# Position bias and first modulation as 32-column products, with eight modulation buffers, on one core

## Chip, cores and metric

One core of a Trainium2 chip runs the whole program as one launch. The metric is the device time of that launch in microseconds; lower is better.

## The reference

Two transformer blocks of two layers each, on one sequence of 512 tokens of width 1024. The first block begins, for each layer, with an adaptive modulation; its first attention branch adds a learned bias that depends on the distance of two positions:

```
mod = silu(c) @ w_ada[l] + b_ada[l]            # w_ada[l]: 1024 x 6144
sh1, sc1, g1, sh2, sc2, g2 = split(mod, 6)
h = x * (1.0 + sc1) + sh1
...
bias = rel_bias[t5_bucket(q_pos[:, :, None] - k_pos)]     # 32 buckets, 8 heads
logits = einsum('bqhd,bqkhd->bqkh', q, k_sel) * a_scale + bias
```

`h` then goes through the projections (`w_in`, 1024 wide), the two attention branches, an output product, a layer norm and a convolutional feed-forward part. The second block (retention, differential attention) doesn't depend on the bias.

## The kernel before

Activations are kept transposed in SBUF, 1024 features as 8 chunks of 128 partitions by 512 tokens. A projection is three fp32r matmuls per 128x128 weight block (L617 to L619): high part of h and high part of w, low part of h and high part of w, high part of h and low part of w. Weights arrive in slots of 128x2048 (1 MB) through two buffers: SP loads `w_raw`, ScalarE writes `w_hi` (`split_hi`), GpSimd the rest `w_lo` (`lo`), and TensorE works off two tiles of 128 outputs per slot.

Each engine has its own instruction stream, written by hand, and semaphores order them. Ahead of the first projection these things happen:

- SP (from L415) loads `c`, constants, the bias table, the positions (`posi`, `qposi`), the parameters `par`, `par2` and weight slots 0 and 1, then works off the stores of the bias (L446 to L455), with the load of x after sixteen of the 32 units. ScalarE, VectorE, GpSimd and TensorE wait for `LOADS`, which counts the parameters too.
- The position bias is made in 32 units G of 16 queries each. The bucket of a distance is a sum of steps: for 32 thresholds x 4 queries on the 128 partitions, a step is 1 where the key position lies at or below a bound. Unit G has four such operands (g = 0 to 3, four queries each) of 128 partitions by n = 128 (G // 8 + 1) keys. ScalarE makes two of them with Sign (L1212), VectorE two with a comparison (L1648). TensorE multiplies each by the table `wb` in three bf16 parts (L674): 12 matmuls of 128 output rows (8 heads x 16 queries, the table zero outside the four queries), all summed in one bank. ScalarE adds a constant and evicts the bank to one of four `stage` buffers (L1219), SP stores it to `bias_scratch` in DRAM (L452). The table itself is made by VectorE with eight small products per part (L1634).
- The first modulation (columns 0 to 2047 of `mod`, the shift and scale that h needs) is summed on VectorE: GpSimd loads w_ada slots 0 to 7 into two `ada_early` buffers (L569), VectorE multiplies each 128x512 piece by its 128 values of silu(c) and adds it up in a bank (`ada_halves`, L1668 and L1670, 32 instructions), and TensorE sums over the partitions with 16 products of one column (`ada_group`, L649). `ada_take` (L1696) adds the bias `b_ada`.
- VectorE computes the angles of the rotary embedding (L1714 to L1723), ScalarE their sines (L1337, L1338).
- For each chunk j of h, ScalarE computes h twice from x, shift and scale: as fp32 in `ht` (L1205) and rounded in `h_hi` (L1206); VectorE subtracts them for `h_lo` (L1727). TensorE's `first_slot` takes the chunks as they come.

The later w_ada slots (8 and on) go through `ada_mid`, two buffers, loaded by SP between the weight slots (L427) and summed on VectorE as above. During the first index projection VectorE also copies the rows kr and iw out of a bank (L1909, L1910), which TensorE's transposes (L820) wait for. In the attention branch the bias of unit (i, h) is read back from DRAM (L489) into four `bias_in` buffers.

The index scores (L843) multiply two heads at a time, one on partitions 0 to 63, one on 64 to 127. L832 are whole-array fp32 products of 512 columns.

Of the kernel before, what the change touches and what calls it, by code (L numbers as in the profile page):

```python
# [62 lines left out]
C_ID, C_ONE, C_MEAN, C_TRI, C_THR, C_INV, C_SGN, C_LNE, C_RMSE, C_SEL, C_HALF, NC = (  # L63
    0, 128, 256, 384, 896, 897, 898, 899, 900, 901, 901 + 64, 901 + 65)
# [5 lines left out]
def tables():  # L70
# [15 lines left out]
    sel = np.zeros((P, 4, 16), np.float32)  # L86
    for p in range(P):
        for g in range(4):
            sel[p, g, 4 * g + p // NBUCKET] = 0.5 if g < 2 else 1.0
    c[:, C_SEL:C_SEL + 64] = sel.reshape(P, 64)  # L90
    c[:, C_HALF] = np.where(r % 16 < 8, 0.5, 0.0)
# [19 lines left out]
def build(nc, a):  # L111
    ctx = ExitStack()
    with ctx:
# [90 lines left out]
        ada_early = [sb(f"ada_early{i}", [P, SLOT], (109 + 8 * i) * KB) for i in range(2)]  # L204
# [5 lines left out]
        step_a = [[sb(f"step_a{i}{g}", [P, S], (175 + 2 * i + g) * KB, bf16) for g in range(2)] for i in range(4)]  # L210
        step_d = sb("step_d", [P, 32, S], 141 * KB, bf16)
        wb = [sb(f"wb{i}", [P, 4, P], (88 + i) * KB, bf16) for i in range(3)]
        relb = sb("relb", [P, 17], 91 * KB)
        relr = sb("relr", [P, 8], 91 * KB + 96)
        relh = sb("relh", [P, 8], 91 * KB + 128, bf16)
        relf = sb("relf", [P, 8], 91 * KB + 160)
        relc = sb("relc", [P, 1], 91 * KB + 192)
        selc = sb("selc", [P, 65], 91 * KB + 256)
        qhalf = sb("qhalf", [P, P], 92 * KB)
        posi = sb("posi", [P, S], 199 * KB, i32)  # L220
        posf = sb("posf", [P, S], 187 * KB)
        qposi = sb("qposi", [P, P], 189 * KB, i32)
        qpos = sb("qpos", [P, P], 189 * KB + 512)
        ang = [sb(f"ang{i}", [P, S], (191 + 2 * i) * KB) for i in range(4)]
        stage = [sb(f"stage{i}", [P, S], (199 + 2 * i) * KB) for i in range(4)]
# [41 lines left out]
        ada_first = [sem(f"ada_first{i}") for i in range(2)]  # L267
# [11 lines left out]
        bias_stored = [sem(f"bias_stored{i}") for i in range(4)]  # L279
        ang_ready = sem("ang_ready")  # L280
        rope_ready = sem("rope_ready")
        h_tmp = sem("h_tmp")
# [88 lines left out]
        bias_dram = nc.dram_tensor("bias_scratch", [H, S, S], fp32, kind="Internal").ap()  # L371
# [37 lines left out]
        LOADS = 16 * 7  # L409
# [4 lines left out]
        def _(sp):  # L414
# [6 lines left out]
            for i in range(DEPTH):  # L421
                sp.dma_start(par[i][:, :], a["par"][i]).then_inc(loaded, 16)
            sp.dma_start(par2[:, :], a["par2"]).then_inc(loaded, 16)
# [22 lines left out]
            for i in range(NB):  # L446
                n = (i + 1) * P
                with sp.Fori(0, 2) as it:
                    for q in range(4):
                        G = i * 8 + q  # L450
                        sp.wait_ge(bias_out, it * 4 + (G + 3))
                        sp.dma_start(bias_dram[:, bass.ds(it * 64 + G * 16, 16), 0:n], stage[q][:, 0:n]  # L452
                                     ).then_inc(bias_stored[q], 16)
                if i == 1:
                    sp.dma_start(x[:, :, :], a["x"]).then_inc(x_loaded, 16)  # L455
            for l in range(DEPTH):
                ws = a["w_stream"][l]
                k = 24 * l + 8
                for m in range(SLOT_IDX, SLOT_QK + 1):
                    if l or m >= 2:  # L460
                        weights(l, m, a["w_ukv"][l] if m == SLOT_UKV else ws[m - (m > SLOT_UKV)])
                    for _ in range((0, 2, 0, 1, 2, 1, 1, 1, 1, 1, 0)[m]):
                        if k == 24 * l + 8:
                            sp.wait_ge(bias_mm, 4 + 8 * NB)
                            if l:
                                sp.wait_ge(tile_done, tdone(l, -1))
# [12 lines left out]
                for u, (i, h) in enumerate(units):  # L479
                    U = aidx(l, 0) * NU + u  # L480
                    if u < 4:
                        if l == 0:
                            for q in range(4):
                                sp.wait_ge(bias_stored[q], 16 * 9)
# [689 lines left out]
        def _(act):  # L1174
# [52 lines left out]
            for i in range(NB - 1):  # L1227
                with act.Fori(0, 2) as it:
                    bias_units(i, it)
                if i < 2:  # L1230
                    split_hi(0, i)
# [1049 lines left out]
```

## Time and profile before

| | |
|---|---|
| median of 3 runs | 2652.95 us (2649.79 to 2653.0) |
| the profiled execution, its time | 2651.0 us |
| its span in the profile | 2649.2 us |
| TensorE matmuls busy | 94% of the span |
| mean granted TensorE clock | 0.968 |
| DMA, mean | 98 GB/s, 259 MB moved |

The profile is of one execution. In it, "busy" of an engine is the time in which one of its instructions ran; PE is TensorE's matmuls, PEld its weight loads, DVE VectorE, ACT ScalarE, POOL GpSimd, SP the engine that issues most DMAs. A name such as L674 is the line of the kernel. An arrow `a<-b` reads "a written from b". "Idle before" is the time in which the engine stood still ahead of these instructions, with what ended it. PEclk is the share of full speed granted to TensorE, 1.00 being 2.4 GHz. Busy times of neighbouring instructions overlap a little, so the distance of two starts is often shorter than one duration.

### The profile page before, as it was taken

Reading aid. Unit: us, or ns where it says so; the run is one execution under the profiler, and the core shown is the slowest. Engines: PE = TensorE matmul, PEld = TensorE weight load, DVE = VectorE, ACT = ScalarE, POOL = GpSimd, SP = SyncE. Lnnn points to the kernel's source line nnn. Section 1 sums busy time; section 2 is a strip of 40 time slices with the busy share of each in tenths; the row PEclk is TensorE's granted clock in tenths of the full one; section 3 lists DMA queues with packets and bytes.
Section 4 is the critical chain, followed back from the end, with each engine's and each line's share of the span. In section 5 each row is a group of like instructions: output and inputs, shape, how many; then the busy total and the mean of one; then the engine's idle time right before and its main releaser. Section 6 shows DMA issues by size and latency. Waiting matters only on the chain.

```text
span 2649.2 us, 32653 instructions
## 1 busy us (share of the span) xinstructions
PE 2484.0 (94%) x11250; PEld 1926.7 (73%) x11252; DVE 1207.1 (46%) x2591; ACT 1042.6 (39%) x1714; POOL 955.9 (36%) x780
## 2 busy tenths in 40 slices
PE   6999999989999989999998999988999989799877
PEld 4667767778888867776777888876788767577555
DVE  7565664654344366557465344134300340534562
ACT  5544434334443244544423444223223442333662
POOL 1234222334444443322243444452444434244211
PEclk9999999989999999999999999999999999899988
DMA  7532123412226253113341222222222202122100
GB/s 257 195 140 79 38 92 114 157 64 95 95 85 225 87 191 127 64 36 97 123 146 70 101 96 80 99 85 74 90 96 98 100 17 83 49 91 80 64 1 32
DMA packets 51728, 259.13 MB, mean 98 GB/s; under 512 B 6112, under 2 KB 16096, under 8 KB 26016
## 3 DMA queue, kind: packets, MB, share of 16 engines
q1 hardware_dynamic: 50464, 249.26, 27.1%
q0 software_dynamic: 1152, 8.39, 0.9%
q8 instruction: 68, 1.11, 0.2%
q14 instruction: 44, 0.36, 0.0%
HBM read 249.11 MB, written 7.34 MB: 97 GB/s over the span
## 4 chain that ended last, share of the span: by engine, by line
PE 88%; DVE 6%; ACT 3%; issue 2%; DMA 1%; POOL 0%; SPq 0%; ACTq 0%; DVEq 0%; POOLq 0%
PE bank L617 24%; PE bank L619 23%; PE bank L618 23%; PE bank L708 3%; PE bank L732 2%; PE bank L721 1%; PE bank L674 1%; PE bank L1045 1%; PE bank L974 1%; PE bank L649 1%; PE bank L843 1%; DMA bias_scratch<-stage 1%; PE bank L1118 1%; PE bank L1034 1%; PE bank L1137 1%
## 5 line engine op out<-in xcount | busy, mean ns | idle before, releaser
L543 POOL TENSOR_TENSOR w_lo<-w_raw,w_hi 128x512 fp32r<-128x512 f32 (+1 forms) x700 | 883.0, 1292 | 1434.4 <-ACT w_hi L1191 887.7
L617 PE MATMUL bank<-h_hi,w_hi 128*128 128x512 f32 x1792 | 734.7, 410 | 32.9 <-DVE h_lo L2054 14.3
L619 PE MATMUL bank<-h_hi,w_lo 128*128 128x512 f32 x1792 | 704.2, 393 | 0.0
L618 PE MATMUL bank<-h_lo,w_hi 128*128 128x512 f32 x1792 | 703.2, 392 | 0.0
L617 PEld LDWEIGHTS bank<-h_hi,w_hi 128*128 128x128 f32 x1792 | 340.2, 190 | 130.6 <-issue 62.3
L618 PEld LDWEIGHTS bank<-h_lo,w_hi 128*128 128x128 f32 x1792 | 340.1, 190 | 72.6 <-issue 8.4
L619 PEld LDWEIGHTS bank<-h_hi,w_lo 128*128 128x128 f32 x1792 | 339.1, 189 | 73.4
L1191 ACT ACTIVATE w_hi<-w_raw 128x2048 fp32r<-128x2048 f32 (+1 forms) x108 | 189.7, 1757 | 280.4 <-PE bank L619 245.5
L2012 DVE SCALAR_TENSOR_TENSOR cv<-bank,par,cv 128x511 f32<-128x511 f32 (+1 forms) x176 | 131.7, 749 | 215.2 <-ACT cv L1440 202.3
L1440 ACT ACTIVATE cv<-bank,par 128x512 f32<-128x512 f32 x88 | 68.3, 779 | 235.3 <-PE bank L619 235.3
L1196 ACT ACTIVATE w_hi<-w_raw 128x2048 fp32r<-128x2048 f32 x76 | 145.1, 1909 | 35.9 <-PE bank L619 35.9
L1270 ACT ACTIVATE L<-L,nmax 128x128 f32<-128x128 f32 (+3 forms) x128 | 72.0, 563 | 186.9 <-DVE nmax L1744 186.4
L617 PE MATMUL bank<-u_hi,w_hi 128*128 128x512 f32 x352 | 138.7, 394 | 0.0
L619 PE MATMUL bank<-u_hi,w_lo 128*128 128x512 f32 x352 | 137.7, 391 | 0.0
L618 PE MATMUL bank<-u_lo,w_hi 128*128 128x512 f32 x352 | 137.5, 391 | 0.0
L617 PE MATMUL bank<-w_hi,h_hi 128*128 128x512 f32 x256 | 100.8, 394 | 0.0
L619 PE MATMUL bank<-w_hi,h_lo 128*128 128x512 f32 x256 | 99.7, 389 | 0.0
L618 PE MATMUL bank<-w_lo,h_hi 128*128 128x512 f32 x256 | 99.6, 389 | 0.0
L1825 DVE SCALAR_TENSOR_TENSOR x<-bank,mod,x 128x512 f32<-128x512 f32 x32 | 24.0, 751 | 161.4 <-PE bank L619 160.3
L2092 DVE TENSOR_TENSOR wt<-bank,decay 128x512 f32<-128x512 f32 (+3 forms) x32 | 13.5, 484 | 172.1 <-PE bank L1034 171.8
L2063 DVE TENSOR_TENSOR rt<-bank,rope 128x512 f32<-128x512 f32 x32 | 22.1, 691 | 127.7 <-PE bank L974 112.5
L618 PEld LDWEIGHTS bank<-u_lo,w_hi 128*128 128x128 f32 x352 | 66.5, 189 | 14.2 <-issue 0.5
(344 smaller groups left out, 3761.0 us busy)
## 6 DMA issues: line engine op xcount, KB each, us to landing
w_raw<-w_stream SPq DMA_DIRECT2D x150, 1024.0 KB, 4.8
w_raw<-w_down SPq DMA_DIRECT2D x32, 704.0 KB, 4.1
ada_mid<-w_ada SPq DMA_DIRECT2D x20, 1024.0 KB, 6.9
ada_last<-w_ada SPq DMA_DIRECT2D x12, 1024.0 KB, 4.8
ada_early<-w_ada POOLq DMA_DIRECT2D x8, 1024.0 KB, 8.1
ada_late<-w_ada SPq DMA_DIRECT2D x8, 1024.0 KB, 6.7
bias_in<-bias_scratch SPq DMA_DIRECT2D x16, 256.0 KB, 2.6
bias_in<-bias_scratch SPq DMA_DIRECT2D x16, 192.0 KB, 2.3
```

The source lines that it names most:

```text
L543: ins = nc.gpsimd.tensor_tensor(w_lo[r][:, part], w_raw[r][:, part], w_hi[r][:, part].bitcast(fp32), ALU.subtract)
L617: nc.tensor.matmul(out, w[0][:, cols], xh, start=first, stop=False)
L618: nc.tensor.matmul(out, w[0][:, cols], xl, start=False, stop=False)
L619: return nc.tensor.matmul(out, w[1][:, cols], xh, start=False, stop=last)
L649: ins = nc.tensor.matmul(banks[bank][:, j:j + 1], ada_acc[late][:, part + j // 4, (j % 4) * P:(j % 4 + 1) * P], ones[:, 0:1], start=True, ...
L708: nc.tensor.matmul(banks[4 + t % 2][:, 0:n], q[rows, hh, i * P:(i + 1) * P], kk[rows, hh, 0:n], start=True, stop=True).then_inc(s_done, 1)
L732: ins = nc.tensor.matmul(banks[u % 2][:, 0:HD], PT[u % 2][:, b * P:(b + 1) * P], v[:, b, h * HD:(h + 1) * HD], start=(b == 0), stop=(b == i))
L1191: A_(w_hi[n % 2][:, 0:cols], w_raw[n % 2][:, 0:cols], ACT.Copy).then_inc(w_hi_done, 1)
L1196: A_(w_hi[n % 2][:, :], w_raw[n % 2][:, :], ACT.Copy).then_inc(w_hi_done, 1)
L1270: A_(L[t % 3][:, 0:n], L[t % 3][:, 0:n], ACT.Exp, bias=nmax[:, t:t + 1], scale=-1.0, accum_out=esum[:, t:t + 1]).then_inc(exp_done, 1)
L1440: A_(cv[s][c][:, :], banks[(t + c) % 4][:, :], ACT.Identity, bias=b, scale=w2).then_inc(conv_first, 1)
L2012: return V.scalar_tensor_tensor(out, banks[(t + c) % 4][:, 0:S - 2 + w], weight, out, ALU.mult, ALU.add)
```

## The change

Bias: each of the four operands of a unit gets its own quarter of the bank's partitions. The table has 32 columns (8 heads x 4 queries) for each kind of operand, and a matmul writes partitions 32g to 32g + 31 of the bank; there are still 12 matmuls per unit, ordered part by part with the four quarters inside. Four banks (2, 3, 6, 7) are used in turn. The operands of a unit lie in one `step` buffer of four; ScalarE makes the first with Sign, VectorE the other three. There are eight `stage` buffers, and the layout of the scratch in DRAM is [128 groups of four queries, 8 heads, 4 queries, 512 keys]. All loops are written out.

Modulation: w_ada slots 0 to 7 have a buffer each (`ada_early`, in the places of h_hi, h_lo and the first gates), and ScalarE issues their loads as its first instructions. silu(c) is widened to 32 equal columns (`c_wide`), and TensorE multiplies with it: four matmuls per slot, one per 512 columns of w_ada, each into its quarter of a bank, after units 3, 6, ..., 24. VectorE copies each finished bank to SBUF (at its units 8, 14, 20, 26), and TensorE picks the columns with 16 one-column products (`C_HOT`), four after units 12, 18, 24 and 26. `ada_group` and `ada_halves` remain for all later slots.

Order: x is loaded ahead of the bias stores. `par` and `par2` have a semaphore of their own, waited for by VectorE after the bias. VectorE computes `ht` for the first h itself (`first_lo`), then `h_lo`; the angles follow after these eight chunks, and ScalarE's sines stand after its second evicted tile. SP's w_ada slots 8 and on wait for the first modulation instead of the last bias matmul.

```diff
-            sp.dma_start(par2[:, :], a["par2"]).then_inc(loaded, 16)
+            sp.dma_start(par2[:, :], a["par2"]).then_inc(par_loaded, 16)
...
+            sp.dma_start(x[:, :, :], a["x"]).then_inc(x_loaded, 16)
+            for i, G in BIAS_UNITS:
                 n = (i + 1) * P
+                sp.wait_ge(bias_out, G + 1)
+                sp.dma_start(bias_dram[4 * G:4 * G + 4, :, :, 0:n].rearrange("a h q n -> (a h q) n"), stage[G % 8][:, 0:n]
+                             ).then_inc(bias_stored[G % 8], 16)
...
-            for k in range(8):
-                if k >= 2:
-                    pool.wait_ge(ada_used, k - 1)
-                pool.dma_start(ada_early[k % 2][:, :], a["w_ada"][k]).then_inc(ada_first[k % 2], 16)
...
+            def bias_unit(i, G):
                 n = (i + 1) * P
+                bank = banks[BIAS_BANKS[G % 4]]
+                if G >= 4:
+                    pe.wait_ge(bias_out, G - 3)
+                pe.wait_ge(step_act, G + 1)
+                pe.wait_ge(step_dve, G + 1)
+                for part in range(3):
                     for g in range(4):
+                        ins = nc.tensor.matmul(bank[32 * g:32 * g + 32, 0:n], wb[part][:, min(g, 1), :],
+                                               step[G % 4][:, g, 0:n], start=(part == 0), stop=(part == 2))
+                ins.then_inc(bias_mm, 1)
+
+            def ada_slot(k):
+                half, s = divmod(k, 2)
+                pe.wait_ge(ada_first[k], 16)
+                if s == 0 and half >= 2:
+                    pe.wait_ge(ada_copied, half - 1)
+                for j in range(4):
+                    ins = nc.tensor.matmul(banks[4 + half % 2][32 * j:32 * j + 32, :], c_wide[:, 4 * s + j, :],
+                                           ada_early[k][:, j * 512:(j + 1) * 512], start=(s == 0), stop=(s == 1))
+                if s:
+                    ins.then_inc(ada_row, 1)
+
+            def ada_columns(half):
+                pe.wait_ge(ada_copied, half + 1)
+                for j in range(4):
+                    ins = nc.tensor.matmul(banks[0][:, 4 * half + j:4 * half + j + 1], ada_rows[half][:, j * P:(j + 1) * P],
+                                           selc[:, 9:10], start=True, stop=True)
+                return ins
+
+            for i, G in BIAS_UNITS:
+                bias_unit(i, G)
+                if G == 3:
+                    pe.wait_ge(c_ready, 1)
+                if G % 3 == 0 and 3 <= G <= 24:
+                    ada_slot(G // 3 - 1)
+                    if G // 3 in (4, 6, 8):
+                        ada_columns(G // 6 - 2)
+                if G == 26:
+                    ada_columns(3).then_inc(ada_sum, 1)
...
+            for k in range(8):
+                act.dma_start(ada_early[k][:, :], a["w_ada"][k]).then_inc(ada_first[k], 16)
             act.wait_ge(loaded, LOADS)
+            A_(c_wide[:, :, :], csilu[:, :].rearrange("p (k o) -> p k o", o=1).broadcast_to([P, 8, 32]), ACT.Silu
+               ).then_inc(act_c, 1)
...
+            for G in range(3):
+                sign(G)
+            for i, G in BIAS_UNITS:
+                if G + 3 < 8 * NB:
+                    sign(G + 3)
+                out(G)
+                if G in (12, 18):
+                    split_hi(0, G // 6 - 2)
...
+            def steps(G):
+                n = (G // 8 + 1) * P
+                if G >= 4:
+                    dve.wait_ge(bias_mm, G - 3)
+                for g in range(1, 4):
+                    ins = V.tensor_scalar(step[G % 4][:, g, 0:n], posf[:, 0:n], qpos[:, 4 * G + g:4 * G + g + 1], None,
+                                          ALU.is_le)
+                ins.then_inc(step_dve, 1)
...
+            for i, G in BIAS_UNITS:
+                steps(G)
+                if G in (8, 14, 20, 26):
+                    ada_copy((8, 14, 20, 26).index(G))
...
+            def first_lo(j):
+                if j >= 2:
+                    dve.wait_ge(h_ready, j - 1)
+                V.tensor_scalar(ht[j % 2][:, :], x[:, j, :], mod[0][:, 8 + j:9 + j], mod[0][:, j:j + 1], ALU.mult, ALU.add
+                                ).then_inc(first_h, 1)
+                dve.wait_ge(first_h, j + 1)
+                dve.wait_ge(h_hid, j + 1)
                 V.tensor_tensor(h_lo[:, j, :], ht[j % 2][:, :], f32(h_hi[:, j, :]), ALU.subtract).then_inc(h_ready, 1)
...
             ada_take(0, 0)
+            dve.wait_ge(ada_mod, 1)
             for j in range(KD):
-                lo_h(0, j)
-            dve.wait_ge(rope_ready, 1)
-            chain(V.tensor_scalar(rope[64:128, S:2 * S], rope[64:128, S:2 * S], ck[64:128, C_SGN:C_SGN + 1], None, ALU.mult))
+                first_lo(j)
+            angles()
+            dve.wait_ge(bias_out, 8 * NB)
```

## Rows read from the trace of the kernel before

**Rows 1.** The page, busy us with share of the span
```profile
PE 2484.0 (94%) x11250; PEld 1926.7 (73%) x11252; DVE 1207.1 (46%) x2591; ACT 1042.6 (39%) x1714; POOL 955.9 (36%) x780
```

**Rows 2.** Chain that ended last, 0 to 140 us: start, us, what
```profile
9.97 1.40 DVE wb L1634 x8
...
44.50 11.41 DMA bias_scratch<-stage
...
62.68 10.31 PE bank L674 x47
72.99 3.46 PE bank L649 x32
...
87.36 0.70 ACT h_hi L1206
```

**Rows 3.** Groups, 0 to 92 us: busy, mean ns, then idle before
```profile
L674 PE MATMUL bank<-step_a,wb 128*128 128x128 bf16 (+3 forms) x190 | 35.2, 324 | 24.1 <-DVE relc L1638 15.7 <-ACT step_a L1212 8.1
...
L1212 ACT ACTIVATE step_a<-posf,qhalf 128x512 bf16<-128x512 f32 (+3 forms) x64 | 32.7, 561 | 1.1 <-DVE qhalf L1628 1.1
L1648 DVE TENSOR_SCALAR step_d<-posf,qpos 128x128 f32 (+3 forms) x64 | 19.8, 383 | 1.7 <-DVE ada_acc_early L1670 0.6 <-PE bank L674 0.6 <-issue 0.4
...
L1670 DVE SCALAR_TENSOR_TENSOR bank<-ada_early,csilu,bank 128x512 f32<-128x512 f32 x24 | 18.1, 756 | 4.7 <-DMA ada_early<-w_ada 3.9
...
L1219 ACT ACTIVATE stage<-bank,relc 128x128 f32<-128x128 f32 (+3 forms) x32 | 16.7, 522 | 28.8 <-PE bank L674 19.2 <-DMA bias_scratch<-stage 9.0
...
L1191 ACT ACTIVATE w_hi<-w_raw 128x2048 fp32r<-128x2048 f32 x2 | 3.8, 1902 | 0.0
```

**Rows 4.** Windows: busy of PE, PEld, DVE, ACT, POOL; PEclk, DMA share, GB/s
```profile
50.00:60.00 10.00, 6.26 (x31) 3.20 (x30) 5.13 (x7) 4.12 (x9) 2.69 (x4) 0.84 0.78 282
...
80.00:89.00 9.00, 8.59 (x39) 3.71 (x37) 0.69 (x1) 6.84 (x11) 0.00 (x0) 0.97 0.29 65
```

**Rows 5.** Timeline, 42 to 123 us: steps, bias matmuls, kr copy, SP issue, transposes
```profile
42.72 6.43 DVE L1648 TENSOR_SCALAR step_d<-posf,qpos 128x512 f32 x16 [0.61 <-PE bank L674]
...
65.06 1.46 PE L674 MATMUL bank<-step_a,wb 128*128 128x512 bf16 x6
...
109.71 0.33 SPq L433 DMA_DIRECT2D w_raw<-w_stream  x1
...
121.23 0.69 DVE L1910 COPY kr_raw<-bank 32x512 f32<-32x512 f32 x1
...
122.67 0.41 PE L820 MATMUL bank<-ck,iw_row 8*128 8x8 f32 x4
```

**Rows 6.** Timeline of TensorE: whole-array fp32 products and row halves
```profile
138.30 1.88 PE L832 MATMUL bank<-c_sq,ck 128*128 128x512 f32 x4
140.11 0.70 PE L843 MATMUL bank<-ik,iq 64*128 64x256 f32 x4
140.74 0.50 PE L617 MATMUL bank<-h_hi,w_hi 128*128 128x512 f32 x1
...
173.06 1.13 PE L843 MATMUL bank<-ik,iq 64*128 64x512 f32 x4
174.12 0.50 PE L617 MATMUL bank<-h_hi,w_hi 128*128 128x512 f32 x1
```

**Rows 7.** Windows of saturated DMA (columns as rows 4); one load's landing
```profile
13.00:15.00 2.00, 0.00 (x0) 0.00 (x0) 1.90 (x13) 0.00 (x0) 0.00 (x0) 1.00 1.00 422
...
48.00:50.00 2.00, 2.00 (x14) 1.22 (x13) 1.96 (x5) 1.85 (x5) 0.00 (x0) 1.00 1.03 438
...
csilu<-c SPq DMA_DIRECT2D x1, 4.0 KB, 1.6
```

**Rows 8.** Timeline of TensorE at the first projection
```profile
88.93 0.47 PE L617 MATMUL bank<-h_hi,w_hi 128*128 128x512 f32 x1 [0.41 <-DVE h_lo L1727]
...
89.24 0.40 PE L618 MATMUL bank<-h_lo,w_hi 128*128 128x512 f32 x1
89.24 0.19 PEld L619 LDWEIGHTS bank<-h_hi,w_lo 128*128 128x128 f32 x1
```

More of the change, by code:

```diff
@@ L85, in tables @@
     c[:, C_RMSE] = RMS_EPS
[L86 to L91, printed above, removed]
+    query = (r[:, None] // NBUCKET == np.arange(4)).astype(np.float32)
+    c[:, C_SEL:C_SEL + 8] = np.concatenate([0.5 * query, query], axis=1)
+    c[:, C_HALF] = np.where(r < 32, 0.5, 0.0)
+    c[:, C_HOT] = np.where(r % 32 == 0, 1.0, 0.0)
     d = np.zeros((P, ND), np.float32)
@@ L266, in build @@
         ada_full = [sem(f"ada_full{i}") for i in range(2)]
-        ada_first = [sem(f"ada_first{i}") for i in range(2)]
+        par_loaded = sem("par_loaded")
+        ada_first = [sem(f"ada_first{i}") for i in range(8)]
+        ada_row = sem("ada_row")
+        ada_copied = sem("ada_copied")
         ada_used = sem("ada_used")
@@ L1176, in _ @@
             act.sem_inc(tile_evac, TILE_PRE)
-            act.sem_inc(bias_out, 2)
-            for i in range(4):
-                act.sem_inc(bias_stored[i], 16)
             n_act = 0
@@ L1215, in out @@
-            def out(i, it, q):
-                n, G = (i + 1) * P, i * 8 + q
-                act.wait_ge(bias_mm, it * 4 + (G + 5))
-                act.wait_ge(bias_stored[q], it * 16 + 16 * (G // 4 + 1))
-                A_(stage[q][:, 0:n], banks[4 + q % 2][:, 0:n], ACT.Identity, bias=relc[:, 0:1]).then_inc(bias_out, 1)
-            def bias_units(i, it):
-                for q in range(4):
-                    steps(i, it, q + 1)
-                    out(i, it, q)
-            steps(0, 0, 0)
@@ L1227, in _ @@
[L1227 to L1231, printed above, removed]
-            bias_units(NB - 1, 0)
-            for q in range(3):
-                steps(NB - 1, 1, q + 1)
-                out(NB - 1, 1, q)
-            act.wait_ge(ang_ready, 1)
-            act.wait_ge(step_act, 64)
+                A_(h_hi[:, j, :], x[:, j, :], ACT.Identity, bias=mod[0][:, j:j + 1], scale=mod[0][:, 8 + j:9 + j]
+                   ).then_inc(h_hid, 1)
@@ L1241, in _ @@
                 make_h(j)
-            out(NB - 1, 1, 3)
             def evac(l, t, out, nb=4, **how):
@@ L1695, in ada_take @@
                 cols = (slice(0, 16), slice(16, 36), slice(36, 48))[group]
-                chain(V.tensor_tensor(mod[l][:, cols], banks[(6, 7, 6)[group]][:, 0:cols.stop - cols.start], par[l][:, cols],
+                chain(V.tensor_tensor(mod[l][:, cols], banks[(6 * l, 7, 6)[group]][:, 0:cols.stop - cols.start], par[l][:, cols],
                                       ALU.add))
@@ L1915, in _ @@
                 if l == 0:
-                    for q in range(4):
-                        dve.wait_ge(bias_stored[q], 16 * 9)
+                    for q in range(8):
+                        dve.wait_ge(bias_stored[q], 16 * 4)
                 for u, (i, p) in enumerate(PAIRS):
```

196 lines of the change are left out of this document (83 added, 113 removed).

## The prediction, made before the kernel with the change had run

> **What bounds the kernel now.** I read the busy shares first, then the chain that ended last, then the windows of its start. TensorE is busy for 94% of the span [rows 1], so behind the start hardly anything but TensorE matters, and the change touches only what lies ahead of the first projection. That starts with the first L617 matmul at 88.93 us [rows 8]; this moment I call M. In the chain [rows 2] the reader is to see that M isn't set by one job but by several in turn: table products on VectorE (three parts of 1.40 us; TensorE waits until 15.7 [rows 3]), bias matmuls, a wait of 11.41 us for a store of the bias (four staging buffers, beside w_ada and x on the same engines), 10.31 us of bias matmuls, 3.46 us of column sums (L649), more bias matmuls, the first h. The groups [rows 3] say who is loaded: bias matmuls 35.2 us in one of their two equal forms; VectorE 19.8 us on its half of the steps and 18.1 on most of the first modulation sums; ScalarE 32.7 on its half and 16.7 on the evictions. No engine needs 89 us by itself; they take turns. The windows [rows 4] show why: DMA moves 282 GB/s in 50 to 60 us, with TensorE idle for a third, and 65 in 80 to 89. w_ada has two buffers, so its transfers come in bursts behind the sums.
>
> **The change part by part.**
> Preparation. Eight table products of a part become two, of about 0.2 us each: 1.0 less, 2.9 in all. The wait for par goes, but the positions, issued just ahead of it, are still needed and now meet eight megabyte loads; I leave VectorE's start where it is. The first bias matmul, held by the table until 15.7, could go at 12.8, and at 13.1 behind the three steps it needs; VectorE begins these at 12.3. ScalarE issues the w_ada loads while it would wait for constants: nothing.
> VectorE. 96 steps for 64: 19.8 x 96/64 = 29.7 us. The sums over w_ada go to TensorE; four copies of a bank come in, 0.69 each by the nearest row, the copy L1910 [rows 5]: 2.8. So 12.3 + 32.5 = 44.8 if it never waits.
> ScalarE. 32 signs for 64, 16.4; evictions 16.7; two w_hi copies 3.8 [rows 3]: 36.9 busy, less about 3 because one begins before the one ahead has ended, and less the three signs made early. It would end near 46.
> TensorE. Twelve matmuls a unit as before, but each on 32 columns of the array and so, by the change's idea, four side by side. No row shows column strips. The nearest rows are the index scores L843, two fp32 products on different 64-row halves: 174.12 - 173.06 = 1.06 us at 512 columns, 0.63 at 256, so 0.43 more per 256 columns, where two whole-array fp32 products (L832) take 1.81 at 512, 0.9 each [rows 6]. Row halves do run side by side, with a fixed 0.2 us. Bounds: four at a time without loss, 3 x 0.22 = 0.65 us a unit at 512 columns and 0.9 a w_ada slot, or none at all, 2.6 and 3.6. I take the near end with that 0.2: 0.9 and 1.1, since it is the same array split the other way. Bias 8 x (0.4 + 0.55 + 0.7 + 0.9) = 20, slots 9, sixteen column products as now 3.5: 33 us, as much as the others, and beside them.
> The Trainium skill has a rule against it ("TensorE: Matmul & The Clock Gate", Part 3): a weight load overlaps running matmuls only where the row group differs, and these strips all use all rows. The trace disagrees for whole-array products: L619's weight load starts at 89.24, with L618's matmul on the same rows running from 89.24 [rows 8]. The same page gives 2.38 times for three column strips; an estimate from it is about 0.9 us a unit, from the rule 2.6.
> Buffers. Eight staging buffers take away the 9.0 us of waits for stores [rows 3]. Eight w_ada buffers let all of it start at once, and here lies what is late next. When the last slot, due at unit 24, is in, the DMA engines have moved w_ada 8.4 MB, two weight slots 2.1, x 2.1, constants 1.2 and 24 to 25 units of bias 3.4: 17.2 MB. Saturated stretches move 422 to 438 GB/s [rows 7]; at 420 that is 41 us. With a first issue near 1.2 and 1.6 us to land (as c's [rows 7]) the last slot is in at 43.8. Earlier slots, one per 5 us while SP's loads take half, come about when wanted; a stall of 2 us that the end doesn't see.
> From the last slot on: its matmuls 1.1 and the copy 0.7. VectorE stands at unit 26 behind that copy, so five units of steps follow, 3 x 0.40 each (6.43/16 [rows 5]): 6.0. Then the last unit's matmuls 0.9, its eviction 0.6, the first h_hi 0.7 [rows 2], the first h_lo 0.7, handovers 0.2. M = 43.8 + 1.8 + 6.0 + 0.9 + 2.2 = 54.7.
> Behind M. h_lo no longer needs ScalarE's second pass, so the first slot's stalls go, about 1 us. Against it TensorE idled more and may enter the slot at 1.2 GHz, where a 512-column matmul takes 0.43 for 0.22; a stretch with idle time was granted 0.84 [rows 4]. I put about 1 us on it: the two cancel. The angles move behind the h_lo's: ten instructions, under 0.7 each, so VectorE's next modulation half starts some 3 us later. Its copy of kr had 0.8 us of slack before TensorE's transposes (121.23 + 0.69 against 122.67), but it stood behind w_ada slot 11, whose load SP held until weight slot 4 could go at 109.71 [rows 5], not behind VectorE: 0, at worst 2. SP now issues the unit stores without loops and waits with the next w_ada loads for the first modulation; POOL's queue loses eight issues and starts its w_lo early; the strided bias reads move the same bytes four ahead: nothing for these, their cover being TensorE's 45 us on the index projection.
> Sum: 88.9 - 54.7 = 34.2 off the profiled execution's 2651.0 (span 2649.2; the runs' median 2652.95 lies 2 above): 2616.8, say 2617.
>
> **Rivals.**
> Serial strips, on the other side. If strips of one row group wait for each other, TensorE bounds: bias 12 x 32 x 0.22 x 320/512 = 53 (320 columns is the mean), 32 slot products of 0.9 = 29, column products 3.5: 85.5 + 13.1 + 2.2 = 100.8 for M, 11.9 later than now: 2663. It decides from where TensorE's work passes 88.9 - 15.3 = 73.6 us, which is where four strips take 3.4 times one (70.1 of 82). For it: no row shows strips, and the rule above. Against: rows 6 and 8. 7%.
> Half clock, or weight loads laid open between strips. TensorE would idle for a quarter to a third of the time, and rows 4 show the clock fall. At 1.2 GHz a 512 unit takes 3 x 0.43 + 0.2 = 1.5 and a slot 2, in all about 50: M near 63, 2625; with open loads too, 2634. Against: a slower TensorE is a busier one. 17%.
> DMA doesn't bind, because w_ada's ring gets more than its share: then ScalarE and VectorE do, at 45 to 46. M about 49, 2611. 16%.
> Something outside the sum: fetching the unrolled code under full DMA load, a late constant, the angles after M. 3 to 12 us above the forecast, 2620 to 2629. 7%.
> Nothing gained because the start is hidden: the chain has it whole. 1%.
>
> **How the numbers follow.** The forecast, 2613 to 2621, has 52%. The range takes in the DMA-free end (2611, less 2 for the uncertain overlap of evictions) and the half-clock cases up to 2634, and leaves out serial strips: 2609 to 2634. Some 0.2%, 5 us, is what a measurement of this kernel can tell from no change; all cases but serial strips and the 1% lie far below 2647.7. Faster 0.92, same 0.01, slower 0.07.
>
> **What would show it.** Right: M between 52 and 57; the four strips of a unit starting within a few ns of each other and rounds about 0.3 us apart; DMA above 400 GB/s from 3 to 43 us; VectorE waiting for TensorE at the copy of unit 26, and TensorE for the last w_ada load; from M to the end as long as before (2649.2 - 88.9 = 2560.3) within 2 us. Wrong: strips 0.2 us apart, ScalarE waiting for TensorE at every eviction, TensorE's products at half clock with M past 60, or a longer stretch behind M.

## The result, and the profile after

The changed kernel takes 2636.19 us (median of 5 runs, 2631.93 to 2638.53), the kernel before 2652.95 (5 runs). The ratio is 0.9935, 95% interval 0.9918 to 0.9953: faster by 17 us, where I had forecast 36 and a range that ended at 2634. The profiled execution took 2632.27 us, its span is 2630.5.

The page's first line, busy us and share of the span, beside [rows 1]:

```profile
PE 2452.3 (93%) x11316; PEld 1904.0 (72%) x11316; DVE 1203.7 (46%) x2585; ACT 1022.0 (39%) x1675; POOL 958.1 (36%) x772
```

TensorE lost 32 us of busy time and the span only 19: it waits more. The chain that ended last, from the start to the first projection, answers to [rows 2]:

```profile
3.37 16.92 DMA qposi<-qpos
20.39 0.44 DVE posf L1634
...
27.04 11.39 DMA bias_scratch<-stage
...
42.37 9.78 DVE step L1656 x18
...
52.75 6.53 DVE step L1656 x18
...
59.88 3.65 DVE step L1656 x3
...
72.64 0.76 PE bank L614
```

M, the start of the first projection, is at 72.64; it was at 88.93 [rows 8] and forecast at 54.7. From M to the end it is 2557.9 us here and 2560.3 before. So nearly the whole error lies ahead of M: 17.9 of some 19 us. (This execution is 3.9 us below the median of its kernel, and M is read from one execution of each kernel, so a few us of a time behind M are the spread of the runs.) The reader is to see three things in the chain: the positions (qposi) take 16.92 us to land, a bias store holds it for 11.39, and between 42 and 63 the steps on VectorE hold it almost alone. The groups of 0 to 75 us, answering to [rows 3]:

```profile
L1656 DVE TENSOR_SCALAR step<-posf,qpos 128x128 bf16<-128x128 f32 (+3 forms) x96 | 36.4, 457 | 0.4 <-PE bank L664 0.4
L664 PE MATMUL bank<-step,wb 128*32 128x128 bf16 (+3 forms) x384 | 21.3, 360 | 35.3 <-DVE step L1656 28.5 <-ACT step L1227 6.5
L1227 ACT ACTIVATE step<-posf,qhalf 128x128 bf16<-128x128 f32 (+3 forms) x32 | 17.5, 556 | 6.6 <-DVE qhalf L1637 6.6
L1235 ACT ACTIVATE stage<-bank,relc 128x128 f32<-128x128 f32 (+3 forms) x32 | 16.8, 526 | 16.3 <-PE bank L664 10.4 <-DMA bias_scratch<-stage 5.7
L545 POOL TENSOR_TENSOR w_lo<-w_raw,w_hi 128x512 fp32r<-128x512 f32 x8 | 16.6, 2106 | 47.6 <-ACT w_hi L1202 47.6
L674 PE MATMUL bank<-ada_early,c_wide 128*32 128x512 f32 x64 | 11.8, 816 | 0.0
...
L1662 DVE COPY ada_rows<-bank 128x512 f32<-128x512 f32 x4 | 2.7, 686 | 6.1 <-PE bank L674 6.1
```

TensorE's part did what the change says: 33.1 us for units and slots, where bias matmuls alone took 35.2. Its waits are for the steps. The mean of a step is 457 ns for 383 before, and GpSimd's subtraction is at 2106 ns. These means hide two kinds of step. The first line has the shortest, the median and the longest step in ns; then GpSimd in the timeline; then three windows with the steps alone (busy of PE, PEld, DVE, ACT; granted clock, DMA share, GB/s):

```profile
L1656 DVE TENSOR_SCALAR step<-posf,qpos x96: 281/380/1494, 24.1 to 68.8; 128x128 bf16<-128x128 f32 x24, 128x256 bf16<-128x256 f32 x24, 128x384 bf16<-128x384 f32 x24, 128x512 bf16<-128x512 f32 x24
43.50 5.47 POOL L545 TENSOR_TENSOR w_lo<-w_raw,w_hi 128x512 fp32r<-128x512 f32 x4 [43.05 <-ACT w_hi L1202]
53.50 11.14 POOL L545 TENSOR_TENSOR w_lo<-w_raw,w_hi 128x512 fp32r<-128x512 f32 x4 [4.53 <-ACT w_hi L1202]
...
43.50:49.00 5.50, 3.13 (x48) 1.63 (x40) 5.50 (x5) 2.60 (x5) 0.58 0.21 72
...
53.50:59.00 5.50, 3.19 (x60) 1.21 (x52) 5.50 (x16) 3.71 (x6) 1.00 0.40 144
59.80:64.60 4.80, 2.16 (x36) 0.70 (x28) 4.80 (x4) 2.04 (x3) 1.00 0.55 206
```

Beside the first four subtractions only five steps fit into 5.5 us. From 53.5 on sixteen fit into the same time, and now it is GpSimd that stands: its fifth subtraction lasts 6.92 us. The other three go at 1.45 each, again beside only four steps in 4.8 us. Of the 96 steps eight are slow, one for each subtraction: seven of 1.42 to 1.49 us and one of 0.90. The others of 384 columns take 0.41, those of 512 some 0.48. So the two engines don't both run somewhat slower; they take turns by whole instructions, and each slow step is about 1.0 us longer. The windows (busy of PE, PEld, DVE, ACT, POOL; granted clock, DMA share, GB/s), answering to [rows 4]:

```profile
10.00:20.00 10.00, 0.00 (x0) 0.00 (x0) 0.00 (x0) 0.62 (x2) 0.00 (x0) 1.00 1.03 413
...
40.00:50.00 10.00, 8.78 (x84) 4.20 (x76) 8.32 (x13) 7.72 (x15) 5.47 (x4) 0.59 0.32 108
```

From 10 to 20 us the DMA engines are full and nobody computes; from 40 on they have little to do. The small loads tell why (SyncE's queue, KB, us to landing):

```profile
ck<-consts SPq DMA_DIRECT2D x1, 450.5 KB, 7.9
...
posi<-pos SPq DMA_DIRECT2D x1, 256.0 KB, 14.7
...
qposi<-qpos SPq DMA_DIRECT2D x1, 64.0 KB, 16.9
...
selc<-consts SPq DMA_DIRECT2D x1, 5.0 KB, 10.1
relb<-rel SPq DMA_DIRECT2D x1, 8.5 KB, 12.3
```

With their issues at 1.21, 1.67, 2.14, 2.88 and 3.37 these land at 9.1, 11.8, 14.4, 17.6 and 20.3: one every 2.7 us (the first of posi and qposi after 3.2), whether it has 5 KB or 256.

### The profile page after: what moved, and what is told of

Its sections match the earlier page's. It is cut to its first block, busy times and chain, and to the rows that moved or that the text cites. A ratio compares the mean times of both kernels' runs of the same rounds, so it can differ in the third digit from the quotient of the medians.

```text
span 2630.5 us, 32212 instructions
## 1 busy us (share of the span) xinstructions
PE 2452.3 (93%) x11316; PEld 1904.0 (72%) x11316; DVE 1203.7 (46%) x2585; ACT 1022.0 (39%) x1675; POOL 958.1 (36%) x772
## 4 chain that ended last, share of the span: by engine, by line
PE 87%; DVE 7%; ACT 3%; issue 2%; DMA 1%; POOL 0%; SPq 0%; DVEq 0%; ACTq 0%; POOLq 0%
PE bank L614 24%; PE bank L616 24%; PE bank L615 24%; PE bank L720 3%; PE bank L744 2%; PE bank L733 1%; PE bank L1059 1%; PE bank L988 1%; DVE step L1656 1%; PE bank L857 1%; PE bank L646 1%; PE bank L1132 1%; PE bank L1048 1%; DMA qposi<-qpos 1%; PE bank L1151 1%
```

## The experiments

All times are medians; the kernel before, run beside each group, stood between 2650.6 and 2653.0. M is read from each profile.

| kernel | M | us | ratio to before, 95% |
|---|---|---|---|
| changed kernel | 72.64 | 2636.19 | 0.9918 to 0.9953 |
| late w_ada | 68.80 | 2632.21 | 0.9909 to 0.9942 |
| late x | 68.50 | 2633.77 | 0.9914 to 0.9947 |
| GpSimd waits | 70.08 | 2636.89 | 0.9927 to 0.9960 |
| all three | 61.71 | 2627.30 | 0.9892 to 0.9925 |
| rows of 2 KB | 73.65 | 2636.92 | 0.9936 to 0.9966 |
| 2 KB, late w_ada | 76.41 | 2638.94 | 0.9933 to 0.9967 |
| 2 KB, all three | 68.48 | 2632.73 | 0.9912 to 0.9945 |
| GpSimd issues, 2 KB | 63.47 | 2627.16 | 0.9896 to 0.9929 |
| GpSimd issues, 8 KB | 61.59 | 2624.25 | 0.9888 to 0.9923 |
| GpSimd's ring takes all | 63.77 | 2627.84 | 0.9904 to 0.9931 |
| that, two and two steps | 69.60 | 2636.96 | 0.9937 to 0.9968 |
| changed, two and two steps | 75.89 | 2642.06 | 0.9961 to 0.9980 |
| GpSimd's ring, 16 stages | 54.71 | 2620.56 | 0.9861 to 0.9891 |
| changed, 16 stages | 68.13 | 2635.01 | 0.9922 to 0.9949 |

**Late w_ada.** ScalarE issues its eight loads only when the constants and the positions have landed.
```diff
+            act.wait_ge(loaded, LOADS)
+            act.wait_ge(pos_loaded, 32)
             for k in range(8):
                 act.dma_start(ada_early[k][:, :], a["w_ada"][k]).then_inc(ada_first[k], 16)
-            act.wait_ge(loaded, LOADS)
```


> The eight w_ada loads are issued only when constants and positions have landed. M is the start of the first projection matmul (72.64 in the changed kernel's profile). Theory A (the late positions cost the start): VectorE begins at 7 to 9 us instead of 20.4; the first stores of the bias now meet w and x in SP's ring, so the wait for a store grows from 5.7 to about 10; M falls by 7 to 9, time by 7 to 9 us against the changed kernel. Theory B (w_ada is what ends last; the start has slack as I predicted): M falls by less than 3, or rises, since w_ada starts 6 us later. Theory C (only VectorE and GpSimd disturbing each other is lost): M unchanged.


VectorE started at 7.00 instead of 20.39, selc landed in 3.0 us. Yet M moved by 3.8 only, where 7 to 9 were expected: the chain's next piece was the store.
```profile
3.09 3.81 DMA qposi<-qpos
16.61 17.56 DMA bias_scratch<-stage
```
The late start is real and w_ada's early issue makes it, but of the 13.4 us most is taken back behind the stores.

**Late x.** x is issued behind the first eight bias stores.
```diff
+                if G == 8:
+                    sp.dma_start(x[:, :, :], a["x"]).then_inc(x_loaded, 16)
                 sp.wait_ge(bias_out, G + 1)
```


> x is issued behind the first eight bias stores instead of ahead of them; w_ada as in the changed kernel. Theory A: the wait of ScalarE for the first stores (5.7 us of idle) goes to under 1 us, start stays at 20.4 or falls by 1 to 2 (x is behind it in the ring, so hardly), M falls by 4 to 6. Theory B (the DMA engines' total decides): the same bytes in another order, M within 2 us of 72.6.


No store is left in the chain, ScalarE's waits for stores fell from 5.7 to 2.1 us, and M by 4.1, as expected. A part of what was won met GpSimd: all eight subtractions now fall on the steps of 384 columns, whose mean went from 578 to 749 ns.

**GpSimd waits.** Its subtractions of the first two weight slots wait until VectorE has made all steps.
```diff
+            pool.wait_ge(step_dve, 8 * NB)
             lo(slot_no(0, 0))
             lo(slot_no(0, 1))
```


> GpSimd makes the low parts of weight slots 0 and 1 only after VectorE's last step. Theory C (VectorE's steps and GpSimd's subtractions slow each other): a step of 384 columns has 0.41 us throughout instead of 1.22 in the stretch with GpSimd busy, one of 512 some 0.45; a GpSimd subtraction 1.26 instead of 2.1; VectorE's steps end 6 to 7 us earlier, and M falls by 4 to 5, no more because the low part of slot 0 (5.0 us) now ends last. Rival (the steps were slow from DMA traffic or because they wait for TensorE at half clock): steps stay slow around 43 to 49 us, M rises by 5.


The steps by form, in this kernel and in the changed one:
```profile
L1657 DVE TENSOR_SCALAR step<-posf,qpos 128x512 bf16<-128x512 f32 x24 | 9.7, 476 | 0.0
L1657 DVE TENSOR_SCALAR step<-posf,qpos 128x384 bf16<-128x384 f32 x24 | 8.2, 413 | 1.0 <-PE bank L665 0.9
```
```profile
L1656 DVE TENSOR_SCALAR step<-posf,qpos 128x512 bf16<-128x512 f32 x24 | 13.1, 620 | 0.0
L1656 DVE TENSOR_SCALAR step<-posf,qpos 128x384 bf16<-128x384 f32 x24 | 12.1, 578 | 0.0
```
So GpSimd beside them costs the steps 7.3 us in the changed kernel, and no slow step is left without it; the rival is out. The steps' end came at 64.3 instead of 69.2, but TensorE then waited 4.7 us for w_lo. M fell by 2.6 instead of 4 to 5, and the time not at all: as an edit alone it gains nothing.

**All three**, with GpSimd's wait ahead of the second slot only.


> All three: w_ada behind the positions, x behind eight bias stores, and GpSimd's low part of slot 1 (not of slot 0) behind VectorE's last step. If the three losses add up as separate terms: start at 8, no wait for stores, half the disturbance left: M near 72.6 - 12 - 5 - 3 = 52 to 55, the value I had predicted, time 17 to 20 us under the changed kernel, some 35 under the kernel before. If w_ada's last slot binds instead: M 55 to 60, TensorE or VectorE waiting for ada_early.


M fell by 10.9 us, to 61.71, as much as by the three alone together (10.5), and the time by 8.9. The 52 to 55 expected were missed. Two pieces were left, seen in the chain:
```profile
6.79 0.39 ACTq L1214
...
11.72 0.46 ACTq L1214
12.21 1.28 ACT L1215
...
17.30 14.71 DMA bias_scratch<-stage
```
ScalarE issues eight loads for 5.4 us before its first sign, and a store still takes 14.0 us at the median, though no x is ahead of it.

**Rows of 2 KB.** Do small transfers wait by rows? w_ada's first slots lie in four pieces in DRAM, so that a row of a transfer has 2 KB instead of 8. The other two are this with the late w_ada, and this with all three.
```diff
-                act.dma_start(ada_early[k][:, :], a["w_ada"][k]).then_inc(ada_first[k], 16)
+                act.dma_start(ada_early[k][:, :].rearrange("p (j c) -> p j c", j=4), a["w_ada_first"][k].rearrange("j p c -> p j c")).then_inc(ada_first[k], 16)
```


> The only edit: the first eight w_ada slots lie in DRAM in four pieces, so that a load writes rows of 2 KB instead of 8 KB per partition; bytes, issue and order stay. In the changed kernel the six small loads land about 2.7 us apart whether they hold 5 KB or 256 KB. Theory D (the rings of SP and ScalarE take turns by row, so eight rows per engine wait for eight w_ada rows of 8 KB): the turn becomes four times shorter, qposi lands 4 to 7 us after its issue instead of 16.9, VectorE begins at 8 to 10 instead of 20.4; w and x, still 8 KB rows, get the larger share, so the stores behind them wait less; M 54 to 60 instead of 72.6, time 10 to 17 us under the changed kernel. Rival (engines share by bytes, or the small loads just queue in a saturated memory): qposi lands after 15 us or more, M within 2 us of 72.6.

> Rows of 2 KB and the w_ada loads behind the landed positions. Beside the run with late w_ada alone (M 68.8, a wait of 17.6 us for a store). Theory D: a store of eight rows per engine no longer waits for rows of 8 KB of w_ada, the 64 KB stores land in under 8 us where they took 15.7, that wait falls under 6 us, M 54 to 58. Rival (stores wait because w and x lie ahead of them in their own ring): they still take over 12 us, M above 63.

> Rows of 2 KB, w_ada behind the positions, x behind the first eight stores, the low part of weight slot 1 behind VectorE's last step. If theory D and the disturbance by GpSimd are the whole of what my prediction missed, M comes to where it had it: 51 to 56, some 20 us less than the changed kernel, ratio to the kernel before 0.987 or lower. If something else binds (the last w_ada slot, TensorE's clock): M 57 to 62, as with all three other edits at rows of 8 KB (61.7).


The small loads, in the first of the three:
```profile
qposi<-qpos SPq DMA_DIRECT2D x1, 64.0 KB, 8.4
...
selc<-consts SPq DMA_DIRECT2D x1, 5.0 KB, 6.8
relb<-rel SPq DMA_DIRECT2D x1, 8.5 KB, 7.2
```
With issues at 1.67, 2.14 and 3.47 selc, relb and qposi land at 8.5, 9.3 and 11.9, posi between them at 11.0: steps of 0.8 to 1.7 us instead of 2.7 to 3.2. VectorE started at 11.95 (8 to 10 expected), and stores of 64 KB landed in 6.3 to 6.5 us, not 10 to 16, in all three. The bytes of every transfer are the same; only w_ada's rows are shorter. (The rate fell a little: 352 GB/s from 6 to 10 us for 420 in the changed kernel, 389 for 409 from 10 to 14.) So a transfer waits a turn for each of its rows, behind a row of the other ring, that is, of the queue of another issuing engine. The Trainium skill ("DMA: Bandwidth & Descriptors", Queues, rings and completion order) has the DMA engines go round between queues at the granularity of a packet, of some 9 to 17 descriptors. The round is what is seen; the turn here is shorter than that: 128 rows are eight for each of sixteen engines, 2.7 us are 0.33 for each, and one 8 KB row at 413 GB/s over sixteen engines takes 0.32.

Against the same edits with 8 KB rows no time was won, for a reason I had not thought of. With w_ada late the stores landed in 6.5 us, as that theory had it, but M was 76.4, where it had 54 to 58; with all three edits it was 68.5 for 51 to 56. The chain of the first of these kernels:
```profile
7.81 4.06 ACTq L1210
...
11.89 12.75 ACTq L1210
...
27.07 1.28 ACT L1212
```
With four times as many rows a single issue held ScalarE for 12.75 us, and it was free at 27.07 (at 29.81 and 24.76 in the other two). The first three issues, with little ahead of them, took 0.53 at most: here an issue of many rows into a queue with much ahead of it isn't asynchronous.

**GpSimd issues.** GpSimd, which is idle then, issues the w_ada loads behind the positions; x behind the eighth store, the second slot's subtractions behind the steps. Once with 2 KB, once with 8 KB rows.
```diff
-            for k in range(8):
-                act.dma_start(ada_early[k][:, :], a["w_ada"][k]).then_inc(ada_first[k], 16)
...
+            pool.wait_ge(loaded, LOADS)
+            pool.wait_ge(pos_loaded, 32)
+            for k in range(8):
+                pool.dma_start(ada_early[k][:, :], a["w_ada"][k]).then_inc(ada_first[k], 16)
             lo(slot_no(0, 0))
+            pool.wait_ge(step_dve, 8 * NB)
             lo(slot_no(0, 1))
```


> Edit: GpSimd instead of ScalarE issues the eight loads of w_ada, behind the loads that the positions need; rows of w_ada are 2 KB long; the load of x stands behind the first eight bias stores; GpSimd's subtractions of the second quarter wait for VectorE's 32nd step. Theory (each small transfer waits for its turn behind rows of the large ones, and ScalarE was held in its own issue): VectorE starts near 7, ScalarE's first sign near 9.5, the 64 KB stores land in under 8 us, and the first projection matmul starts at 52 to 57 us, where my forecast had it; the kernel takes 2615 to 2622 us. Rival (the total of the w_ada bytes, VectorE beside GpSimd, or TensorE's clock binds by then): first projection matmul at 58 to 68, 2624 to 2633 us, with the stores' landing short all the same.

> Edit: as e8_pool_2k, but with the 8 KB rows of w_ada as in the changed kernel; it differs from e4_all in the engine alone that issues the loads of w_ada. Theory: ScalarE's first sign at about 9.5 instead of 14.1 us, but the 64 KB stores still take about 14 us to land, since each of their rows waits behind an 8 KB row; the first projection matmul starts at 57 to 61, 1 to 4 us before e4_all's 61.7, and the kernel takes 2622 to 2626 us. Rival (the issue on ScalarE cost nothing, the stores alone bind): 61 to 63 and no difference to e4_all.


ScalarE's first sign came at 8.5 and 8.4 instead of 14.1, and M barely moved against all three together (61.7): 63.5 and 61.6. For 8 KB rows M is the rival's: a freed ScalarE reaches the store wait sooner, and waits for stores 9.6 us instead of 6.9.
```profile
22.89 18.57 DMA bias_scratch<-stage
```
For 2 KB rows my 52 to 57 was wrong. First, GpSimd's ring did not carry 2 KB pieces: the profile has 2176 packets for the eight loads, where ScalarE's ring had 4224, so that a packet had 4 KB, and the stores of 64 KB landed some 1.5 us one behind the other. Second, x. Stores of 64 KB landed in 7.8 us, those of 128 KB, which stand behind x, in 16.7: the chain waits for one 16.8 us, from 25.20 on. Shorter turns don't help whoever is second in his own ring.

**GpSimd's ring takes all.** It issues the two weight slots and x too; SyncE's ring holds small loads and stores alone.
```diff
             for k in range(8):
                 pool.dma_start(ada_early[k][:, :], a["w_ada"][k]).then_inc(ada_first[k], 16)
+                if k in (2, 4):
+                    m = k // 2 - 1
+                    pool.dma_start(w_raw[m][:, 0:SLOT], a["w_stream"][0, m]).then_inc(w_first[m], 16)
+            pool.dma_start(x[:, :, :], a["x"]).then_inc(x_loaded, 16)
```


> Edit: e9_pool_8k (GpSimd issues the eight loads of w_ada behind what the positions need, rows of 8 KB, the subtractions of the second quarter behind VectorE's 32nd step), and GpSimd's ring also takes the two first loads of w_raw (behind the third and the fifth w_ada slot) and the load of x (last), so that SyncE's ring holds nothing but the small loads and the bias stores. In e9_pool_8k ScalarE waited 9.6 us for bias stores, the chain 18.6, although its stores of 64 KB had no x ahead of them; those of 128 KB did. Theory (the stores stand behind x and w_raw in one ring, in order; a turn of a row behind 8 KB rows costs a third of a microsecond only): a 64 KB and a 128 KB store land in 3 to 6 us, ScalarE waits under 2 us for stores, the first projection matmul starts at 52 to 56 and the kernel takes 2615 to 2620 us, what my forecast said. Rival (the turns by row behind w_ada hold the stores, whatever stands in their ring): stores still 12 us to landing, first projection matmul at 59 to 62, 2622 to 2626 us. Second rival: the stores land soon, but VectorE, TensorE's half clock or the last loads bind next: 56 to 60.


My theory fell and the rival held for the stores: those of 64 and 128 KB took 14.9 and 14.1 us with nothing large ahead of them. M and the time (63.8, 2628) lie even above the rival's. ScalarE's evictions in the timeline, with what they waited for:
```profile
20.32 0.47 ACT L1240 ACTIVATE stage<-bank,relc 128x256 f32<-128x256 f32 x1 [1.64 <-DMA bias_scratch<-stage]
...
23.69 0.47 ACT L1240 ACTIVATE stage<-bank,relc 128x256 f32<-128x256 f32 x1 [2.50 <-DMA bias_scratch<-stage]
...
26.33 0.47 ACT L1240 ACTIVATE stage<-bank,relc 128x256 f32<-128x256 f32 x1 [1.77 <-DMA bias_scratch<-stage]
...
28.96 0.47 ACT L1240 ACTIVATE stage<-bank,relc 128x256 f32<-128x256 f32 x1 [1.76 <-DMA bias_scratch<-stage]
```
After the first, a buffer comes free every 2.63 us. Packets of the two queues in 12 to 36 us of the same kernel:
```profile
q0 software_dynamic: 1314, 9.58, 95.2%
q1 hardware_dynamic: 1054, 0.48, 6.9%
```
The stores have 45% of the packets and 5% of the bytes. In 18 to 31 us, where ScalarE waits for one store after the other, it is 701 packets against 698: one for one. This is the missing row of my sum: while rows of 8 KB flow, a store of 64 KB costs 2.63 us (the small loads of 5 to 256 KB cost 2.7 to 3.2 in the changed kernel), 32 stores at that pace would cost 84, and only buffers uncouple the units from them. When the large loads are through, near 40 us, the next stores land some 0.4 us apart.

**Two and two steps.** The second step operand goes back to ScalarE, once in the kernel above and once in the changed one.
```diff
-                A_(step[G % 4][:, 0, 0:n], posf[:, 0:n], ACT.Sign, scale=-1.0, bias=qhalf[:, 4 * G:4 * G + 1]
-                   ).then_inc(step_act, 1)
+                for g in range(2):
+                    ins = A_(step[G % 4][:, g, 0:n], posf[:, 0:n], ACT.Sign, scale=-1.0,
+                             bias=qhalf[:, 4 * G + g:4 * G + g + 1])
+                ins.then_inc(step_act, 1)
...
-                for g in range(1, 4):
+                for g in range(2, 4):
```


> Edit: e10_pool_all with two of the four step operands on each engine, as before the change, in the new layout. What the third operand on VectorE is worth once nothing else holds the strip: VectorE has 32 steps fewer (about 15 us at its mean of 0.41 us and the slowed ones), ScalarE 32 signs more (18 us at 0.55). Theory (in e10_pool_all VectorE's line is the full one: 96 steps in 32 us and its end ahead of M, ScalarE has room): with 2 and 2 ScalarE holds 64 signs (35 us), 32 evictions (17 us) and 3.8 of copies, 56 us from 8.4 on, so it ends at 64 or later, and the first projection matmul is 6 to 10 us later than in e10_pool_all; 2622 to 2629 us. Rival (the step operands are not what binds): within 2 us of e10_pool_all.

> Edit: the changed kernel with two of the four step operands on each engine, nothing else: the part of the change that moved a third one to VectorE is undone alone. In the changed kernel VectorE starts at 20.4, makes 96 steps in about 45 us, and its last steps end ahead of the first projection matmul (72.6). Theory (VectorE beside GpSimd is the last of the lines there): without 32 steps VectorE loses 32 of 96 steps, but ScalarE, which starts at the same time, gets 32 signs (18 us) on top of its 38 us, so it ends at 20.4 + 56 + its store waits of 5.7, past 80: M at 76 to 82, 3 to 9 us slower than the changed kernel, 2639 to 2646 us. Rival (VectorE beside GpSimd costs more than ScalarE's signs): M at 68 to 73, equal or faster.


M is 5.8 and 3.3 us later (6 to 10 and 3 to 9 expected), the time 9 and 6; the first kernel's 2637 lies 8 us above what I had expected, and no run shows why. In the changed kernel ScalarE's steps then hold 23% of the chain's first 85 us. So the third step on VectorE is worth some 3 us of M and 6 of the time there. The rival, that ScalarE's signs cost less than VectorE beside GpSimd, is out.

**Sixteen stages.** Twice as many staging buffers, in the kernel whose loads GpSimd issues and in the changed one.
```diff
-        stage = [sb(f"stage{i}", [P, S], (179 + 2 * i if i < 4 else 191 + 2 * i) * KB) for i in range(8)]
+        stage = [sb(f"stage{i}", [P, S], (163 + 2 * i if i < 12 else 175 + 2 * i) * KB) for i in range(16)]
...
-                if G >= 8:
-                    act.wait_ge(bias_stored[G % 8], 16 * (G // 8))
+                if G >= 16:
+                    act.wait_ge(bias_stored[G % 16], 16)
```


> Edit: e10_pool_all with sixteen stage buffers for the bias strips instead of eight. In e10_pool_all nothing but the small loads stood ahead of the stores in SyncE's ring, and they still landed 2.64 us one behind the other (ScalarE resumed at 20.3, 23.7, 26.3, 29.0, 31.6 us), the spacing of the small loads in the changed kernel (2.7): a store of 128 rows gives each of sixteen DMA engines 8 rows, and each waits for one 8 KB row of the other ring, 0.33 us. Theory (as many stores as fit into the time of the bulk loads, some 12 by 42 us, and eight more buffered, are all the units that can be done by then): with sixteen buffers ScalarE waits under 4 us for stores instead of 14.2, the first projection matmul starts at 53 to 57 instead of 63.8, and the kernel takes 2615 to 2621 us. Rival (the bytes of w_ada or VectorE beside GpSimd bind just behind): 58 to 62, 2621 to 2626 us.

> Edit: the changed kernel with sixteen stage buffers instead of eight, nothing else (w_ada still from ScalarE, at once). Theory: of the three late things of the changed kernel this takes away the store wait alone (11.4 us in the chain, 5.7 of ScalarE's idle time); the start at 20.4 and VectorE beside GpSimd stay, so the first projection matmul goes from 72.6 to 67 to 70 and the time falls by 2 to 6 us, 2630 to 2634. Rival (VectorE beside GpSimd takes the gain, as in e2_late_x, where the store wait was gone and M went to 68.5 but the steps slowed): 70 to 73, no change.


In the first M falls from 63.77 to 54.71, and the time to 2620.56, both as expected, 15.6 us below the changed kernel and the best of all. No store is left in its chain:
```profile
9.79 14.68 DMA ada_early<-w_ada
...
36.96 6.52 DVE step L1665 x18
43.49 0.60 DVE ada_rows L1671
44.09 3.21 DVE step L1665 x9
...
50.14 1.28 DVE mod L1715
...
54.71 0.51 PE bank L623
```
In the changed kernel alone the same edit makes no difference that can be told (2635.01 for 2636.19). M is 4.5 us earlier in its profile and the store is gone from the chain, but VectorE's steps hold 38% of the chain's first 75 us there: it starts at 20.32, waits 1.3 us for TensorE in all, and the eight subtractions again bring its 384-column steps to a mean of 749 ns. So with the stores' wait gone VectorE bounds the changed kernel, and the store wait only just reaches past it. The two causes lie over each other, as the kernels with one cause taken away show.

## Why the forecast was wrong

**Preparation: the step that failed first.** I wrote that the positions "are still needed and now meet eight megabyte loads; I leave VectorE's start where it is". The meeting was seen and priced at nothing, with no row behind it and no bound above. It cost VectorE's start 12.2 us (20.39 for 8.18). The same sum reckoned with full DMA engines until 43.8; that they would be full for the positions too should have been a term. The page's landing times before (csilu 1.6 us [rows 7]) held for idle engines only.

**VectorE: 12.3 + 32.5 = 44.8 "if it never waits".** It began its steps at 24.1 and ended at 69.2, 45.1 us for 32.5. The steps took 36.4 for 29.7: GpSimd's subtractions, which the change starts early, as I wrote and priced at nothing, fall on them. The other 5.9 us it waited, nearly all at the copies, 4.80 of them where a store held ScalarE. Late start 11.8, slower steps 6.7, waits 5.9, less the 6.8 that my sum left free between VectorE (44.8) and the steps behind the last slot (51.6): 17.6. From the last step to M it took 3.4 us for 3.1, and that makes the 17.9 by which M is late.

**Buffers: "eight staging buffers take away the 9.0 us of waits for stores".** With eight, stores still held ScalarE for 5.7 us and the chain for 11.39. A bound from above lay in [rows 2]: the store of 11.41 us beside w_ada and x was there before, I named its cause and then let a count of buffers remove it. The kernels with all loads on GpSimd's ring show the rule, 2.63 us for each store of 64 KB beside 8 KB rows, and sixteen buffers are what my sum needed.

**ScalarE issues its loads "while it would wait for constants: nothing".** Right in the changed kernel, where the constants are late anyway; with the late w_ada the eight issues cost 4.5 us (5.4 with all three edits), and with short rows 18 and more.

**TensorE: right.** A unit of twelve matmuls at 512 columns takes 0.83 us (0.9 forecast), and eight matmuls of w_ada 1.04 (1.1 for a slot), at full clock; the four strips of a round start within 34 ns of each other, the rounds 0.22 us apart. Strips of 32 columns run side by side although they use the same rows, so the serial rival is out. By the rule that I quoted from the Trainium skill ("TensorE: Matmul & The Clock Gate", Part 3) I had estimated 2.6 for the 0.83, and the trace disagrees with it.

**Half clock: in part.** The granted clock was 0.59 in 40 to 50 us, behind TensorE's waits for the late start and the stores, and TensorE entered the first slot at half clock, where the first six matmuls start 0.43 apart. It followed from the waits; M was past 60, as that rival said, for other reasons.

**DMA: the rate right, the binding wrong.** 399 to 450 GB/s stood from 4 until about 35 us. The last slot bound nothing. **Something outside the sum**, the 7% rival, comes nearest in kind: "a late constant". Its time, 2620 to 2629, still supposed one mishap, not three.

**Behind M: right.** 2557.9 us for 2560.3, and some 4 more at the median of the runs. Over all kernels here it was 2557.8 to 2565.5. From M to the transposes [rows 5] it is 34.15 in the changed kernel and 34.45 in the best; the rest of these two's difference lies late, where the granted clock differs by some hundredths (0.95 and 0.93 in 2200 to 2500 us).

**The sum itself.** With the start, the stores and the overlap with GpSimd mended, M came at 54.71, where the forecast had 54.7, and the time at 2620.56 for 2617. That M agrees so closely is luck in part: the last copy at 43.49 (44.9 in my sum) and VectorE's last step at 50.0 (51.6) are near what I had, but ahead of it w_ada came later (its slot held the chain until 24.5), and the first h took longer beside GpSimd (4.6 us from the last step to M for 3.1). That the terms left out were these three is what the runs show.

## What to carry to other kernels

A small transfer beside large ones is priced by its rows, not its bytes: count its rows for each DMA engine, take one large row's time for each, and ask who waits for it. Loads that everything waits for go out and land first, large ones behind them and from an engine with nothing to do; stores under load need as many buffers as units are made in that time. And when a change brings work of GpSimd forward, look for what VectorE does in that stretch: here each subtraction cost it about 1 us, or waited 6.9 us itself.

## What was not expected of the hardware

- Turns by row: small loads landed 2.7 to 3.2 us apart beside 8 KB rows and 0.8 to 1.7 beside 2 KB rows; stores of 64 KB (128 rows) 2.63 us apart beside 8 KB rows and some 1.5 beside packets of 4 KB.
- An issue that blocks: with 512 rows for each load instead of 128, one issue on ScalarE took 12.75 us; the eight with 8 KB rows took 4.4 to 5.4 together. On GpSimd the same issues took some 750 ns each, and 530 with 8 KB rows, with no such stop.
- VectorE and GpSimd take turns by whole instructions where steps and subtractions meet: in the changed kernel eight of 96 steps took 0.90 to 1.49 us instead of 0.41 to 0.48, one for each subtraction, and one subtraction took 6.92 us beside a run of sixteen fast steps, where the mean of the whole kernel is 1.30. Without subtractions beside them (GpSimd waits) no step was slow.
